# Branch A's scores and value up-projection as three fp32r products instead of one fp32 product

## The reference

```python
q_lat = jnp.einsum('bshd,hdc->bshc', a_q.reshape(B, S, A_HEADS, HEAD_DIM), w_uk[l])
kv_lat = rmsnorm(a_kv, g_kv[l])
...
logits = jnp.einsum('bqhc,bqkc->bqhk', ql, kv_sel) * ATTN_SCALE + bias
p = jax.nn.softmax(logits, axis=-1).astype(kv_sel.dtype)
return jnp.einsum('bqhk,bqkc->bqhc', p, kv_sel)          # o_lat
...
o_a = jnp.einsum('bshc,hce->bshe', o_lat, w_uv[l]).reshape(B, S, -1)
```

## Time and profile before

| | |
|---|---|
| median of 3 runs | 1016.07 us (1014.48 to 1016.63) |
| the profiled execution's own time | 1017.55 us |
| its span, first to last instruction | 1015.4 us |
| TensorE busy | 987.6 us, 97% of the span |
| VectorE, ScalarE, GpSimd busy | 48%, 38%, 10% |
| mean granted TensorE clock | 0.997 of full speed |

### The profile page before, as it was taken

The page is one execution under the profiler, slowest core; times in us unless marked ns, Lnnn a source line. Parts: engine busy times, 40 slices in busy tenths (PEclk is TensorE's granted clock), DMA queues, the critical chain, the costliest instruction groups (busy, mean ns, idle before and its releaser), DMA issues.

```text
span 1015.4 us, 12602 instructions
## 1 busy us (share of the span) xinstructions
PE 987.6 (97%) x4879; PEld 803.3 (79%) x4879; DVE 483.5 (48%) x822; ACT 381.1 (38%) x675; POOL 99.8 (10%) x138
## 2 busy tenths in 40 slices
PE   5899999999999999999999999999999999999997
PEld 3678988878877777778888888988888888788885
DVE  2754687843335335664647374733343343231323
ACT  6244523245555656652222233542232222221222
POOL 3210000000045431200000002000000000000401
PEclk9999999999999999999999999999999999999999
DMA  8866134321330201064555662123334434222312
GB/s 302 277 215 190 54 113 139 93 79 43 104 103 25 64 22 42 32 208 137 183 193 171 206 224 100 63 83 103 103 107 150 147 112 139 88 104 83 125 42 83
DMA packets 88162, 123.11 MB, mean 121 GB/s; under 512 B 4824, under 2 KB 69941, under 8 KB 87986
## 3 DMA queue, kind: packets, MB, share of 16 engines
q1 hardware_dynamic: 87442, 115.98, 35.0%
q0 software_dynamic: 528, 6.22, 2.0%
q10 hardware_dynamic: 144, 0.26, 0.1%
HBM read 119.77 MB, written 8.45 MB: 126 GB/s over the span
## 4 chain that ended last, share of the span: by engine, by line
PE 92%; issue 3%; DVE 1%; ACT 1%; DMA 1%; POOL 1%; SPq 0%; POOLq 0%; ACTq 0%; DVEq 0%
PE tile_ps L826 19%; PE tile_ps L828 18%; PE tile_ps L827 18%; PE t_ps L1049 2%; PE s_ps L1031 2%; PE o_ps L1078 2%; PE o_ps L1225 1%; PE o_ps L1226 1%; PE tile_ps L1226 1%; PE s_ps L1226 1%; PE t_ps L1226 1%; PE o_ps L1227 1%; PE tile_ps L1225 1%; PE s_ps L1225 1%; PE t_ps L1225 1%
## 5 line engine op out<-in xcount | busy, mean ns | idle before, releaser
L826 PE MATMUL tile_ps<-h_hi,w_hi 128*128 128x512 f32 x736 | 292.6, 398 | 0.4
L828 PE MATMUL tile_ps<-h_hi,w_lo 128*128 128x512 f32 x736 | 287.1, 390 | 0.0
L827 PE MATMUL tile_ps<-h_lo,w_hi 128*128 128x512 f32 x736 | 286.8, 390 | 0.0
L1702 DVE TENSOR_TENSOR w_lo<-w_raw,w_hi 128x2048 fp32r<-128x2048 f32 (+2 forms) x62 | 135.8, 2190 | 162.2 <-ACT w_hi L1334 162.0
L826 PEld LDWEIGHTS tile_ps<-h_hi,w_hi 128*128 128x128 f32 x736 | 138.2, 188 | 37.1 <-issue 8.6
L828 PEld LDWEIGHTS tile_ps<-h_hi,w_lo 128*128 128x128 f32 x736 | 138.1, 188 | 29.6
L827 PEld LDWEIGHTS tile_ps<-h_lo,w_hi 128*128 128x128 f32 x736 | 138.3, 188 | 26.9 <-issue 0.2
L1334 ACT ACTIVATE w_hi<-w_raw 128x2048 fp32r<-128x2048 f32 (+2 forms) x62 | 111.5, 1798 | 41.1 <-PE s_ps L1227 9.0
L1699 DVE TENSOR_TENSOR t_lo<-t_raw,t_hi 128x2048 fp32r<-128x2048 f32 (+1 forms) x15 | 32.8, 2183 | 85.8 <-ACT t_hi L1332 85.8
L1472 ACT ACTIVATE nl<-nl,cst 128x256 f32<-128x256 f32 (+3 forms) x81 | 43.1, 532 | 50.0 <-DVE cst L1898 49.9
L1332 ACT ACTIVATE t_hi<-t_raw 128x2048 fp32r<-128x2048 f32 (+1 forms) x15 | 27.0, 1800 | 81.7 <-PE s_ps L1227 53.5
(11 more groups left out here) (366 smaller groups left out, 1679.2 us busy)
## 6 DMA issues: line engine op xcount, KB each, us to landing
w_raw<-in_w_in_dram SPq DMA_DIRECT2D x31, 1024.0 KB, 5.5
w_raw<-in_w_gate_up_dram SPq DMA_DIRECT2D x22, 1024.0 KB, 7.1
ada<-in_w_ada_dram SPq DMA_DIRECT2D x12, 1024.0 KB, 5.4
t_raw<-in_w_down_dram SPq DMA_DIRECT2D x10, 1024.0 KB, 5.0
row_copies<-row_flat POOLq DMA_DIRECT2D x1, 5632.0 KB, 21.1
ada<-in_w_ada_dram SPq DMA_DIRECT2D x8, 640.0 KB, 14.4
ada<-in_w_ada_dram SPq DMA_DIRECT2D x8, 512.0 KB, 4.4
ada<-in_w_ada_dram SPq DMA_DIRECT2D x8, 384.0 KB, 9.3
```

Of the source, the lines that this page charges most:

```text
L826: pe.matmul(dst[0:mw, :], wh, x_hi[:, kx, :], start=start, stop=False)
L827: pe.matmul(dst[0:mw, :], wh, x_lo[:, kx, :], start=False, stop=False)
L828: mm = pe.matmul(dst[0:mw, :], wl, x_hi[:, kx, :], start=False, stop=stop)
L1702: dve.tensor_tensor(w_lo[s][:, 0:kt, :], w_raw[s][:, 0:kt, :], w_hi[s][:, 0:kt, :].bitcast(F32), ALU.subtract) \
```

## The change

Both of branch A's remaining fp32 products get the treatment of the projections. For the scores, the latents `kv_T` and the latent queries `qlat` are kept as fp32r high parts, with new low parts `kv_lo` and `q_lo`; for the up-projection, `olat` and `w_uv` are split into `olat_hi`, `olat_lo`, `uv_hi`, `uv_lo`. One matmul becomes three. The products of the probabilities with the latents (L1078) and the latent queries themselves (L1092) stay fp32.

```diff
-                    mm = pe.matmul(ps[:, 0:w], qlat[h % 3][:, i * P:(i + 1) * P], kv_T[:, 0:w], start=True, stop=True)
+                    if v == 40:
+                        pe.wait_ge(kv_moved, 1)
+                    q_h, q_l = (q[:, i * P:(i + 1) * P] for q in (qlat[h % 3], q_lo[h]))
+                    pe.matmul(ps[:, 0:w], q_h, kv_T[:, 0:w], start=True, stop=False)
+                    pe.matmul(ps[:, 0:w], q_l, kv_T[:, 0:w], start=False, stop=False)
+                    mm = pe.matmul(ps[:, 0:w], q_h, kv_lo[v >= 40][:, 0:w], start=False, stop=True)
...
-                pe.matmul(tile_ps[b][0:DH, :], w_uv[:, h, :], olat[:], start=True, stop=True) \
+                if h == 0:
+                    pe.wait_ge(uv_split, 1)
+                pe.matmul(tile_ps[b][0:DH, :], uv_hi[:, h, :], olat_hi[:], start=True, stop=False)
+                pe.matmul(tile_ps[b][0:DH, :], uv_hi[:, h, :], olat_lo[:], start=False, stop=False)
+                pe.matmul(tile_ps[b][0:DH, :], uv_lo[:, h, :], olat_hi[:], start=False, stop=True) \
...
+            def latent_hi(h):
+
+                t = ATT_TILE["qlat", h]
+                wait_tile_made(act, t)
+                act.activation(qlat[h % 3][:], tile_ps[t % 2][:], ACT.Copy).then_inc(qlat_hi_made, 1)
...
-                    evacuate(ATT_TILE["qlat", qlat_at(v)[0]], qlat[qlat_at(v)[0] % 3][:, :])
+                    latent_hi(qlat_at(v)[0])
...
-                        act.activation(olat[:], o_ps[g % 2][:], ACT.Copy).then_inc(olat_in, 1)
+                        act.activation(olat_hi[:], o_ps[g % 2][:], ACT.Copy).then_inc(olat_hi_made, 1)
...
-                        evacuate(ATT_TILE["qlat", h], qlat[h % 3][:, :])
+                        latent_hi(h)
+                if v == 36:
+                    act.wait_ge(wu_in, 32)
+                    act.activation(uv_hi[:], w_uv[:], ACT.Copy).then_inc(uv_hi_made, 1)
+                    act.activation(kv_lo[1][:], kv_lo[0][:].bitcast(F32), ACT.Copy).then_inc(kv_moved, 1)
...
-            dve.tensor_copy(kv_T[:], o_ps[1][:]).then_inc(kv_ready, 1)
+            link(dve.tensor_copy(kv_T[:], o_ps[1][:]))
+            dve.tensor_tensor(kv_lo[0][:], o_ps[1][:], kv_T[:].bitcast(F32), ALU.subtract).then_inc(kv_ready, 1)
...
+                    if MIX_A <= p < MIX_B and p % 4 == 3:
+                        g, h = p // 4, (p - MIX_A) // 4
+                        dve.wait_ge(olat_hi_made, h + 1)
+                        dve.tensor_tensor(olat_lo[:], o_ps[g % 2][:], olat_hi[:].bitcast(F32), ALU.subtract) \
+                            .then_inc(olat_in, 1)
+                for h in qlat_at(v):
+                    t = ATT_TILE["qlat", h]
+                    dve.wait_ge(qlat_hi_made, h + 1)
+                    dve.tensor_tensor(q_lo[h][:], tile_ps[t % 2][:], qlat[h % 3][:].bitcast(F32), ALU.subtract) \
+                        .then_inc(tile_out[t % 2], 1)
+                if v == 37:
+                    dve.wait_ge(uv_hi_made, 1)
+                    dve.tensor_tensor(uv_lo[:], w_uv[:], uv_hi[:].bitcast(F32), ALU.subtract).then_inc(uv_split, 1)
```

More of the change, by code:

```diff
@@ L246, in hybrid_block @@
         aq_T = place("aq_T", R + 0, [P, 4, S])
-        kv_T = place("kv_T", R + 8, [P, S])
+        kv_T = place("kv_T", R + 8, [P, S], F32R)
+        kv_lo = [place(f"kv_lo{b}", R + at, [P, S], F32R) for b, at in enumerate((31, 49))]
         kv_nat = place("kv_nat", R + 10, [P, NBLK, P])
@@ L266, in hybrid_block @@
         olat = place("olat", R + 31, [P, S])
+        olat_hi = place("olat_hi", R + 31, [P, S], F32R)
+        olat_lo = place("olat_lo", R + 65, [P, S], F32R)
         junk_b = place("junk_b", R + 101, [P, S])
@@ L279, in hybrid_block @@
         tm = [place(f"tm{b}", R + 113.25 + 2 * b, [P, S]) for b in range(2)]
-        qlat = [place(f"qlat{b}", R + 117.25 + 2 * b, [P, S]) for b in range(2)]
-        qlat.append(aq_T[:, 0, :])
+        qlat = [place(f"qlat{b}", R + at, [P, S], F32R) for b, at in enumerate((117.25, 119.25, 0))]
+        q_lo = [place(f"q_lo{b}", R + at, [P, S], F32R) for b, at in enumerate((97, 99, 57, 59, 61, 63))]
+        q_lo += q_lo[2:4]
         nlb = [place(f"nlb{b}", R + 113.25 + 2 * b, [P, S]) for b in range(3)]
         w_uv = place("w_uv_sb", R + 121.25, [P, A_H, DH])
+        uv_hi = place("uv_hi", R + 67, [P, A_H, DH], F32R)
+        uv_lo = place("uv_lo", R + 121.25, [P, A_H, DH], F32R)
         mg_lo = place("mg_lo", R + 0, [P, KT, S], F32R)
@@ L402, in hybrid_block @@
         olat_in = sem("olat_in")
+        olat_hi_made = sem("olat_hi_made")
+        qlat_hi_made = sem("qlat_hi_made")
+        uv_hi_made, uv_split, kv_moved = sem("uv_hi_made"), sem("uv_split"), sem("kv_moved")
         cols_ready = sem("cols_ready")
```

## The result

The changed kernel takes 1020.88 us, the median of 8 runs (1018.91 to 1023.15), against 1016.9 us (8 runs beside them, 1014.48 to 1017.88). The ratio is 1.0044, with a 95% interval of 1.0033 to 1.0054: slower by about 4.5 us. The forecast was 1021.1 us, 5.0 more than a median of 1016.1. The total came out right; the waits and TensorE's saving did not, the clock was left out, and these errors cancelled.

The account below looks back on a forecast made before the run. The prediction took TensorE, busy 97% of the span, as the bound, each new wait paid in full. Waits of +8.3 us less 3.3 of TensorE savings gave +5.0: 1021.1 us, range 1018.5 to 1023.6.

Parts of the forecast that it names:

- The 128-wide price: Cost of a 128-wide fp32r matmul on TensorE, taken as 0.112 us, so three for one fp32 score cost 0.11 more.
- three quarters at every width: The skill's rule that three fp32r products cost three quarters of one fp32; a 128-wide score would gain 0.06 us.
- the up-projection, 512 wide too: -0.19: Each of eight up-projections was to save TensorE 0.19 us, 1.52 in all, priced like a 512-wide score.
- Place (1): Steps 43 to 45: `olat_lo` delays branch C's chain, so step 44's shift comes 2.65 us later; TensorE idles almost 3 us.
- The clock rival: The almost 3 us idle before step 45's products takes TensorE's clock down, up to 1.7 us more: 1022.8; chance 0.10.
- Place (2): Step 45: `q_lo` frees the bv tile's bank 0.75 us later; with the late shift before it, +3.4 us together.
- Place (3): Steps 37 and 38: ScalarE's two copies delay head 2's query copy, then `q_lo` delays the bv tile's bank; +1.1 us.
- Places (4) and (5): Steps 48, 56: `olat_lo` delays bank clearing before up-projections, +1.0 us each; steps 52, 53: exponential and `q_lo` late, +1.8.
- Steps 40 and 60 nothing: Up-projections there follow `olat` at once, but `olat_lo` would be ready about when TensorE arrives: no added wait.
- savings pass, waits hide: Rival: TensorE's 3.8 us saving comes through and subtractions hold up nothing: 1012.3 us, or about 1013; chance 0.05 (faster).
- partly hidden: Rival: the summed waits come out at half, +4.2 instead of +8.3 us, net +0.8: 1016.9 us; chance 0.10.
- dear 128-wide products: Rival: 128-wide fp32r matmuls cost as much as fp32, three 0.666 us instead of 0.336: +1.3, 1022.4 us; chance 0.05.

Follow-up runs that it names:

- kernel without low parts: Changed kernel with the high part in place of each low part, no subtractions or waits for them, output not the layer's; -5.0 us against before (0.9951).
- filled kernel: Changed kernel plus eight 128-wide fp32 filling matmuls in step 45's idle stretch, no wait changed; +3.0 us against the kernel before.
- chain first: Changed kernel with branch C's chain of small VectorE operations ahead of `olat_lo` instead of behind it; +1.3 us against the kernel before.
- scores only: Changed kernel with its up-projection undone, one fp32 product again; scores stay three fp32r products; +0.5 us against the kernel before (1.0005).
- up-projection only: Changed kernel with its scores undone, one fp32 product again; up-projection stays three fp32r products; +4.0 us against the kernel before.
- all late: Changed kernel with `olat_lo` and `q_lo` behind later shifts, some up-projections and queries moved, `uv_hi` and `uv_lo` copied later; -2.6 us against before.
- queries' low parts late: Changed kernel with latent queries of heads 2, 4, 6 a step earlier and `q_lo` behind the next shift; +2.2 us against before.
- split queries: Kernel before, all fp32, with latent queries of heads 2, 4, 6 at the ends of steps 36, 44, 52; +0.9 us (1.0009).

## Why the prediction was right, and where its terms were off

The profiled execution's stretch grew by 5.23 us. It splits into idle time +5.73, 0.66 for a pair of matmuls that no idle row shows (below), the fall of the clock +3.29 and TensorE's saving -4.45. The clock's share is what remains: the work of 77.01 less the 0.66, less the 73.06 of the kernel without low parts; the filled kernel gives 2.8 for the same and the one with the chain first 2.86, so it is known to some half a microsecond. The forecast had waits of 8.3, a saving of 3.3 and a clock that stays up.

So the mechanism is shown: subtractions in VectorE's fixed order make TensorE wait for more than the cheaper products save. That the total came out within a quarter of a microsecond is luck. The waits were forecast 1.9 us too long and the saving 1.1 too small, and a fall of the clock worth about 3 us, which the sum left out, made up for both. Where the clock stayed up, in the filled kernel, the stretch grew by 2.93 and not by 5. One sign of the forecast failed with it: TensorE's idle time was to be 2.8 + 8 to 9 us and was 8.58 in all. The others came in their places, though mostly smaller.

**TensorE's saving: mechanism right, size off.** -3.3 forecast, -4.45 measured in the stretch, where my prices give 3.3 as well (2.1 for its 31 scores, six times 0.19). The 128-wide price was right: rows 312.82 and 312.94 are 0.12 apart, taken 0.112. But "three quarters at every width" does not hold at 128, where three products cost more than the one: from the score of step 32 to that of step 33 it is 0.98 us with scores only and 0.89 before. (The sum counts two such scores, of steps 40 and 60; the sentence on the three quarters speaks of four.) The failed term is "the up-projection, 512 wide too: -0.19": it saves 0.50. I took the price of a 512-wide score for a matmul with 64 columns of weights.

**Place (1).** Forecast 2.65 us more until the shift of step 44, and almost 3 us idle. The idle time was 2.47, 2.06 more than the earlier trace rows: `olat_lo` ended as worked out, but branch C's chain took 2.22 us (314.20 to 316.42) and not 2.74, so that the shift came 1.90 us later than before. The same operations stood in it; most of the difference is one of them (L1972, now L2015), 0.51 us before and 0.17 after; before and after:

```profile
312.06 0.51 DVE L1972 TENSOR_TENSOR cst<-cst 128x16 f32<-128x16 f32 x1
```

```profile
314.49 0.18 DVE L2015 TENSOR_TENSOR cst<-cst 128x16 f32<-128x16 f32 x1
```

Why it was shorter stays open. The kernel with the chain first shows this order as the cause of the idle stretch.

**The clock rival.** I gave it 0.10 and at most 1.7 us, taken from the 3.4 us at half speed of the earlier trace rows. That is the step that failed most: the profiled execution lost about 3 to it, near twice the bound, since the clock was at half for 6.8 us. It seems not to happen in every execution: of the eight, the three with a mean clock of 0.992 took 1021.9 to 1023.2 us, the two with 0.996 and 0.997 took 1018.9 and 1019.5. Those means don't say where the clock fell, so that the two kept it up in place (1) is inferred. If they did, the change costs about 2.3 us without the fall (their mean, 1019.2, against 1016.9). Nor does the length of the idle stretch alone decide: after 1.67 us in step 53 of the changed kernel no fall, after 1.70 there in the kernel with the up-projection only one of 3.4 us. What decides stays open.

**Place (2).** +0.75 for `q_lo` is right, 0.76 where place (1) doesn't cover it (scores only, chain first). In the changed kernel it shows 0.15, under the slow clock. Together (1) and (2) were +2.2 idle in place of +3.4, and some 3 of clock. The bv tile of step 46, the point to which the +3.4 was reckoned, came at 322.20 instead of 318.19.

**Place (3).** Forecast +1.1, measured 0.96: 0.07 before the products of step 37, 0.23 for `q_lo`, and 0.66 in the pair of latent queries. I had ScalarE's two copies hold back its copy of head 2's queries. What they held back first was the clearing of the bv bank, for which the second query waits. In the changed kernel:

```profile
295.21 0.62 ACT L1575 ACTIVATE uv_hi<-w_uv_sb 128x512 fp32r<-128x512 f32 x1
...
295.73 0.62 ACT L1576 ACTIVATE kv_lo<-kv_lo 128x512 fp32r<-128x512 f32 x1
296.01 1.79 PE L1106 MATMUL tile_ps<-aq_T,w_uk_sb 64*128 64x512 f32 x4
296.25 0.37 ACT L1359 ACTIVATE bv<-tile_ps 128x256 f32<-128x256 f32 x1
296.68 0.29 PEld L1106 LDWEIGHTS tile_ps<-aq_T,w_uk_sb 64*128 64x128 f32 x2 [0.38 <-ACT bv L1359]
```

The group lasts 1.79 us and not 1.13, and TensorE is never idle in it. The second query's weights load at 296.68, just after the bank is cleared and 0.67 behind the first query, so the two no longer run side by side. Only the length of the group and the weight loads (PEld) show it.

**Places (4) and (5).** Steps 48 and 56: +0.68 of idle time each (1.20 less 0.52), forecast 1.0; the up-projection of step 48 starts 2.93 us after its step's score and not 2.06, +0.87, but TensorE's own work in front of it also grew. Place (5), where the idle times stand before the products of step 53 and the bv tile of step 54: 1.67 - 0.62 + 0.69 = +1.74, forecast 1.8. "Steps 40 and 60 nothing" holds: no idle row stands there.

The rival "savings pass, waits hide" needed the subtractions off the chain. With the written order they were not; with another order (all late, -2.6 us) the change does gain. The rival "partly hidden" had the waits at half of 8.3; they were 6.4 (5.73 and 0.66). The rival "dear 128-wide products" is refuted.

## What to carry to other kernels

When an edit gives an idle-looking engine a small operation that waits, look at what stands behind it in that engine's fixed order, not at its load: here 0.7 us of subtraction held back 2.2 us of unrelated work, and behind it the shift on which TensorE hung. Price a matmul by a row of its own shape, rows and columns of weights included, and before moving one, look whether its neighbour runs beside it. And count a long idle stretch of TensorE, here 2.5 us, twice: once as waiting and once as the clock that may fall after it.

## What the runs showed of the hardware

- An idle stretch of 2.47 us in a TensorE otherwise 97% busy was followed by 6.8 us at 1.2 GHz, one of 2.50 us (up-projection only) by 3.4 us (PEclk 0.83 over 316 to 326 us). Of the sixteen idle stretches of 1.2 to 1.7 us in branch A of all the profiles, fourteen were followed by none; one of 1.20 (queries' low parts late) and one of 1.70 (up-projection only) by 3.4 us. Filled with matmuls whose results nobody needs, the wait that had given 2.47 us left the clock up.
- Two fp32 matmuls with 64 rows of weights, on different halves of the partitions, took 1.06 us together and one took 1.05. When the second started 0.67 us behind the first, the pair took 1.72.
- An fp32 up-projection with 64 columns of weights cost 0.50 us more than its three fp32r products, a 512-wide score with 128 columns 0.16 (from the score of step 39 to that of step 40, 2.93 us before and 2.77 with scores only).
- The clock near the program's start differs between profiled executions as well: at 0.5 for 3.4 us in the kernel before, for 6.8 in the changed one, and not at all in the kernel before with split queries. That is 1.7 us and more of full speed missing; how much of it a run's time takes is not shown. It is outside the branch A stretch.
